# Layer 0's gate/up product in a hybrid streaming encoder step, rewritten as Strassen's seven block products

## The reference

```python
def swiglu(h, w_in, w_out):
    gu = h @ w_in
    return (jax.nn.silu(gu[..., :D_FF]) * gu[..., D_FF:]) @ w_out

hp = hp + rms_norm(swiglu(rms_norm(hp, g[2]), ffn_w_in[layer], ffn_w_out[layer]), g[3])
```

## Time and profile before

| | |
|---|---|
| median of 3 runs | 1019.76 us (1017.18 to 1019.86) |
| profiled execution, first to last instruction | 1018.8 us |
| TensorE busy | 1003.2 us, 98% |
| VectorE busy | 627.9 us, 62% |
| ScalarE busy | 518.8 us, 51% |
| DMA | 161.77 MB, 159 GB/s over the span |
| mean granted TensorE clock | 0.997 of full |

### The profile page before, as it was taken

How to read it: one execution, slowest core, us unless ns; L and a number is a source line. 1 busy time by engine, 2 the same in 40 slices (tenths; PEclk the granted TensorE clock), 3 DMA queues, 4 the chain that set the end, 5 groups by cost and what they waited for, 6 DMA issues and landing times.

```text
span 1018.8 us, 18393 instructions
## 1 busy us (share of the span) xinstructions
PE 1003.2 (98%) x7578; PEld 972.6 (95%) x7578; DVE 627.9 (62%) x918; ACT 518.8 (51%) x902; POOL 48.4 (5%) x55
## 2 busy tenths in 40 slices
PE   7999999999999999999999999999999999999997
PEld 6799899999999999999999999999999999999886
DVE  5396655878555555544579778798855555444553
ACT  5633665655444444444457655676544444444442
POOL 0081210000000000000000000001000000000000
PEclk9999999999999999999999999999999999999999
DMA  8322131666665555546655476556655555456653
GB/s 277 82 79 84 42 101 46 185 195 180 187 186 169 164 166 165 166 133 182 185 157 162 143 202 196 166 150 203 186 171 166 165 166 155 135 163 178 211 168 134
DMA packets 290516, 161.77 MB, mean 159 GB/s; under 512 B 14522, under 2 KB 281634, under 8 KB 290432
## 3 DMA queue, kind: packets, MB, share of 16 engines
q1 hardware_dynamic: 289968, 160.13, 53.9%
q0 software_dynamic: 224, 0.35, 0.1%
q10 hardware_dynamic: 240, 0.10, 0.0%
HBM read 157.98 MB, written 2.58 MB: 158 GB/s over the span
## 4 chain that ended last, share of the span: by engine, by line
PE 89%; DVE 6%; DMA 2%; ACT 2%; issue 1%; DVEq 0%; ACTq 0%
PE ps L564 29%; PE ps L566 28%; PE ps L565 28%; DVE wlo L1551 2%; DVE tmp L1827 1%; ACT whi L1089 1%; DMA raw<-in_ffn_w_out_dram 1%; DMA gain_rows<-in_norm_g_dram 1%; PE ps L815 1%; PE ps L759 1%; PE ps L650 1%; DMA raw<-in_ffn_w_in_dram 0%; DVE tmp L1813 0%; DMA raw<-in_c_w_dram 0%; DVE h L1817 0%
## 5 line engine op out<-in xcount | busy, mean ns | idle before, releaser
L1551 DVE TENSOR_TENSOR wlo<-raw,whi 128x1024 fp32r<-128x1024 f32 (+2 forms) x322 | 366.4, 1140 | 261.5 <-ACT whi L1089 261.2
L564 PE MATMUL ps<-xhi,whi 128*128 128x256 f32 (+1 forms) x1600 | 466.6, 292 | 1.4 <-DVE xlo L1836 0.9
L566 PE MATMUL ps<-xhi,wlo 128*128 128x256 f32 (+1 forms) x1600 | 460.8, 288 | 0.0
L565 PE MATMUL ps<-xlo,whi 128*128 128x256 f32 (+1 forms) x1600 | 459.8, 287 | 0.0
L1089 ACT ACTIVATE whi<-raw 128x1024 fp32r<-128x1024 f32 (+2 forms) x322 | 313.9, 977 | 224.6 <-PE ps L566 190.9
L564 PEld LDWEIGHTS ps<-xhi,whi 128*128 128x128 f32 x1600 | 300.9, 188 | 3.9 <-issue 2.1
L565 PEld LDWEIGHTS ps<-xlo,whi 128*128 128x128 f32 x1600 | 301.1, 188 | 0.0
L566 PEld LDWEIGHTS ps<-xhi,wlo 128*128 128x128 f32 x1600 | 300.9, 188 | 0.0
L564 PE MATMUL ps<-mhi_b,whi 128*128 128x288 f32 x352 | 105.5, 300 | 0.0
L566 PE MATMUL ps<-mhi_b,wlo 128*128 128x288 f32 x352 | 105.0, 298 | 0.0
L565 PE MATMUL ps<-mlo_b,whi 128*128 128x288 f32 x352 | 103.5, 294 | 0.0
(11 more groups left out here) (234 smaller groups left out, 1029.0 us busy)
## 6 DMA issues: line engine op xcount, KB each, us to landing
raw<-in_ffn_w_in_dram SPq DMA_DIRECT2D x176, 512.0 KB, 3.8
raw<-in_ffn_w_out_dram SPq DMA_DIRECT2D x48, 384.0 KB, 3.4
raw<-in_ffn_w_out_dram SPq DMA_DIRECT2D x48, 320.0 KB, 3.1
raw<-in_ffn_w_out_dram SPq DMA_DIRECT2D x22, 512.0 KB, 4.4
raw<-in_ab_w_in_dram SPq DMA_DIRECT2D x10, 512.0 KB, 5.4
raw<-in_ab_w_out_dram SPq DMA_DIRECT2D x10, 256.0 KB, 2.8
raw<-in_ab_w_out_dram SPq DMA_DIRECT2D x20, 128.0 KB, 3.2
x_tok<-in_x_prompt_dram SPq DMA_DIRECT2D x4, 512.0 KB, 7.4
```

Of the source, the lines that this page charges most:

```text
L564: pe.matmul(out, wh, xh, start=first, stop=False)
L565: pe.matmul(out, wh, xl, start=False, stop=False)
L566: return pe.matmul(out, wl, xh, start=False, stop=last)
L1551: dve.tensor_tensor(wlo[:, s, 0:n], raw[:, m % NRAW, 0:n], whi[:, s, 0:n].bitcast(F32), ALU.subtract)\
```

## The change

Layer 0's gate/up product no longer runs as two halves of the frames with all weights each. Frames (halves 0 and 1), model width (blocks k 0 to 3 and 4 to 7) and columns (gate and up of the same f) make it a 2 x 2 by 2 x 2 block product, done with seven block products of half the depth and half the frames:

- First pass, `fast_first`: unit p(f), the gate weights of f on half 0, in two halves of the depth. The first half's sum is copied to p1 (it is needed again), then the second half completes the gate of half 0. Meanwhile `combinations` builds the sums of x: S1, S2, S3, S4.
- Rest, `fast_rest`: for each f gate and up are loaded once more as a pair. VectorE makes four differences of their halves in t_sum (`first_terms`, `second_term`, `last_term`), split as units ta and tb; the second half of up is unit tc, split straight from `raw`. TensorE does five terms of 12 matmuls: S2 and S1 (ta), S3 (tb), S4 (tc of f - 1, `p3`), and the lower half of x (tb). ScalarE seeds PSUM with p1 (`seed`) and copies the running sum out twice (`keep_sum`); VectorE adds (`up_b`, `first_up`) and multiplies (`other_mult`, `first_mult`).
- `raw` has four slots, all four used by pairs and three by others; each pair takes two, so a pair lies in slots 2 and 3 and the next in 0 and 1.
- For b = 0 the gated values of f below 13 are split in the loop (`inner_high`, `inner_low`); the other nine blocks and all of b = 1 are split in ffn_out(0, 0) (`splits`).
- Small loads share semaphores: the gains wait for two loads, others for six and three. The stage table of (0, 1) is drawn together.

```diff
@@ constants and the table @@
-    (0, 1): {"sum": 1, "spread": 3, "scale": (3, 5, 7, 9), "fold": 11, "pre": 13, "again": 15, "x": (15, 17, 19, 21)},
+    (0, 1): {"sum": 0, "spread": 2, "scale": (2, 3, 4, 5), "fold": 6, "pre": 7, "again": 9, "x": (9, 10, 11, 12),
+             "s1": (11, 13), "s2": (14, 15, 16, 17), "s34": (17, 18)},
-NRAW, NSPLIT = 3, 4
+NRAW, NSPLIT = 4, 4
+FAST = (0,)
+EARLY = 13
@@ the order of the units @@
+        if layer in FAST:
+            seq += [("p", layer, f) for f in range(FC)]
+            for f in range(FC):
+                seq += [("ta", layer, f)] + [("tc", layer, f - 1)] * (f > 0) + [("tb", layer, f)]
+            seq.append(("tc", layer, FC - 1))
+LATE = [(f, min(f + 2, FC)) for f in range(EARLY, FC, 2)]
+PAIRS = [(f, f + 2) for f in range(0, FC, 2)]
+SPLIT_SLOTS = (0, 0, 0, 1, 1, *range(4, 26, 2))
@@ slots of raw @@
+        paired = load[0] in ("gate", "up")
+        if paired != (before in ("gate", "up")):
+            n = 2
+        slots.append(n)
+        holders.append(held[n])
+        held[n] = r
+        n = (n + 1) % (NRAW if paired else NRAW - 1)
...
-            def raw_free(m):
-                if m >= NRAW:
-                    sp.wait_ge(w_lo, m - NRAW + 1)
+            def raw_free(r):
+                if RAW_HOLDER[r] is None:
+                    if RAW_SLOT[r] == NRAW - 1:
+                        sp.wait_ge(w_used, U_OUT + len(OUT_DEPTHS))
+                    return
+                load = LOADS[RAW_HOLDER[r]]
+                if load[0] == "gate":
+                    sp.wait_ge(terms_done, terms(*load[1:]) + 3)
+                else:
+                    sp.wait_ge(w_lo, AT[("tc", *load[1:]) if load[0] == "up" else load] + 1)
@@ start @@
-            pe.wait_ge(gains_loaded, 16)
+            pe.wait_ge(gains_loaded, 32)
@@ TensorE, fast_first @@
+                for f, m in enumerate(P_PASS[layer]):
+                    pe.wait_ge(w_lo, m + 1)
...
+                    if f == 0:
+                        pe.wait_ge(x_lo_done[0], 8 * layer + 1)
+                        half_product(f, range(KC // 4), True, False)
+                        pe.wait_ge(x_lo_done[0], 8 * layer + 2)
+                        half_product(f, range(KC // 4, KC // 2), False, True).then_inc(p1_done, 1)
+                    else:
+                        half_product(f, range(KC // 2), True, True).then_inc(p1_done, 1)
+                        second(f - 1)
+                    run(f)
+                second(FC - 1)
@@ TensorE, fast_rest @@
+                def p3(f):
+                    m = AT["tc", layer, f]
+                    pe.wait_ge(w_lo, m + 1)
+                    pe.wait_ge(up_b_done, n0 + f + 1)
...
+                    term(m, 0, 2 + f % 2, *s4, CUT, False).then_inc(w_used, 1)
+                for f in range(FC):
+                    i = n0 + f
+                    ma, mb = AT["ta", layer, f], AT["tb", layer, f]
+                    pe.wait_ge(w_lo, ma + 1)
+                    pe.wait_ge(p1_seeded, i + 1)
...
+                    term(ma, HALF, f % 2, *s2, n, False).then_inc(sum_done, 1)
+                    if f >= 2:
+                        pe.wait_ge(up_a_done, i - 1)
...
+                    term(ma, 0, 2 + f % 2, *s1, n, True).then_inc(w_used, 1)
+                    pe.wait_ge(w_lo, mb + 1)
+                    pe.wait_ge(sum_kept, 2 * i + 1)
...
+                    term(mb, 0, f % 2, *s3, n, False).then_inc(sum_done, 1)
+                    if f:
+                        p3(f - 1)
+                    pe.wait_ge(sum_kept, 2 * i + 2)
+                    term(mb, HALF, f % 2, *a22, n, False).then_inc(w_used, 1)
+                p3(FC - 1)
@@ ScalarE, fast_rest @@
+                for f in range(FC):
+                    if f:
+                        gate_other(f - 1)
+                    else:
+                        s_high(layer, 3)
+                    if f < FC - 1:
+                        seed(layer, f + 1)
+                    inner_high(f - 2)
+                    keep_sum(f, 0)
+                    if f < FC - 1:
+                        hi_part(AT["ta", layer, f + 1])
+                    keep_sum(f, 1)
+                    hi_part(AT["tc", layer, f])
+                    if f < FC - 1:
+                        hi_part(AT["tb", layer, f + 1])
@@ VectorE @@
+            def first_terms(layer, f):
+                i = terms(layer, f)
+                g, u = LOAD_AT["gate", layer, f], LOAD_AT["up", layer, f]
+                dve.wait_ge(w_loaded[RAW_SLOT[g]], loaded(g))
+                dve.wait_ge(w_loaded[RAW_SLOT[u]], loaded(u))
...
+                dve.tensor_tensor(t[:, 0], pair_w[:, 1], pair_w[:, :, 0], ALU.subtract).then_inc(terms_done, 1)
...
+                for f in range(FC):
+                    lo_part(AT["tb", layer, f])
+                    if f:
+                        other_mult(f - 1)
+                    else:
+                        s_low(layer, 3)
+                    if f < FC - 1:
+                        first_terms(layer, f + 1)
+                    inner_low(f - 2)
+                    if f < FC - 1:
+                        second_term(layer, f + 1)
+                        lo_part(AT["ta", layer, f + 1])
+                        last_term(layer, f + 1)
+                    dve.wait_ge(sum_kept, 2 * (n0 + f) + 2)
+                    dve.tensor_tensor(up_b(f), e3(f), flat(2 + f % 2, 0, TOK - CUT), ALU.add).then_inc(up_b_done, 1)
+                    if f:
+                        first_up(f - 1)
+                    lo_part(AT["tc", layer, f])
+                    if f:
+                        first_mult(f - 1)
```

More of the change, by code:

```diff
@@ L117, in unit_sequence @@
     for layer in range(2):
-        for b in range(2):
+        if layer in FAST:
[3 more added lines that the diff above has]
+            seq.append(("tc", layer, FC - 1))
+        for b in range(2 if layer not in FAST else 0):
             for u in range(2 * FC):
@@ L147, in inner, with split_count @@
     return (2 * layer + b) * FC + f
+LATE = [(f, min(f + 2, FC)) for f in range(EARLY, FC, 2)]
+PAIRS = [(f, f + 2) for f in range(0, FC, 2)]
+SPLIT_SLOTS = (0, 0, 0, 1, 1, *range(4, 26, 2))
+def split_count(layer, b, f):
+    before = sum(SPLITS if n in FAST else 2 * FC for n in range(layer))
+    if layer not in FAST:
+        return before + b * FC + f + 1
+    if b:
+        return before + EARLY + len(LATE) + f // 2 + 1
+    return before + (f + 1 if f < EARLY else EARLY + (f - EARLY) // 2 + 1)
+SPLITS = EARLY + len(LATE) + len(PAIRS)
 def z_count(s, d):
@@ L177, in unit_columns, with load_sequence, load_of, raw_slots @@
     return UNIT
+def load_sequence():
+    seq = []
+    for unit in UNITS:
+        if unit[0] == "ta":
+            seq += [("gate", *unit[1:]), ("up", *unit[1:])]
+        elif unit[0] not in ("tb", "tc"):
+            seq.append(unit)
+    return seq
+LOADS = load_sequence()
+LOAD_AT = {load: r for r, load in enumerate(LOADS)}
+def load_of(m):
+    unit = UNITS[m]
+    return LOAD_AT[("up", *unit[1:]) if unit[0] == "tc" else unit]
+def raw_slots():
+    slots, holders, held = [], [], [None] * NRAW
+    n = 0
+    for r, load in enumerate(LOADS):
+        before = LOADS[r - 1][0] if r else load[0]
+        paired = load[0] in ("gate", "up")
[5 more added lines that the diff above has]
+        n = (n + 1) % (NRAW if paired else NRAW - 1)
+    return slots, holders
+RAW_SLOT, RAW_HOLDER = raw_slots()
+def terms(layer, f):
+    return 3 * (FAST.index(layer) * FC + f)
 def out_order(e):
     return [step for step, (_, b) in enumerate(OUT_STEPS) if b in (None, OUT_STEPS[e][1])].index(e)
[L185 to L194 removed]
+def load_dmas(r):
+    if U_IN + 6 <= r < U_IN + 10:
+        return 2
+    return 3 if LOADS[r][0] == "out" else 1
+def loaded(r):
+    return 16 * sum(load_dmas(j) for j in range(r + 1) if RAW_SLOT[j] == RAW_SLOT[r])
 def stepper(chain):
@@ L1508, in last_half, with splits @@
+            def splits(layer):
+                for step, slot in enumerate(SPLIT_SLOTS):
+                    yield slot
+                    split_high(layer, step)
             def last_half():
@@ new lines, in fast_first @@
+            def fast_first(layer, run):
+                for f, m in enumerate(P_PASS[layer]):
+                    run(f)
+                    if 0 < f < FC - 3:
+                        lo_part(m + 3)
+                    elif f == FC - 3:
+                        run(LAST)
+                        first_terms(layer, 0)
+                        second_term(layer, 0)
+                        lo_part(AT["ta", layer, 0])
+                    elif f == FC - 2:
+                        last_term(layer, 0)
@@ L2035, in pooling, with splits @@
+            def splits(layer):
+                for step, slot in enumerate(SPLIT_SLOTS):
+                    yield slot
+                    split_low(layer, step)
             def pooling(b):
```

527 lines of the change are left out of this document (424 added, 103 removed).

## The result

The changed kernel takes 1066.41 us (median of 4 runs, 1065.26 to 1068.35), the kernel before 1019.81 beside it (1017.18 to 1020.15): a ratio of 1.0471, 95% interval 1.0452 to 1.0491. The forecast was 1046, range 1032 to 1062. The sign came as forecast, and so did the closed loop behind it. The size did not: +46.6 us where +26 stood, and outside the range, most of it through a part that was costed at nothing.

What follows compares the result with a forecast made beforehand. TensorE, busy 98%, was taken as the bound. First pass to 253.8, then 12.25, 192.1, 13.8 and 5.0 give 477.0 against 451.6; with the front +26.0, span 1044.8, plus 1.0 for the median: 1046 us, range 1032 to 1062.

Steps and rivals of the forecast that it cites:

- the closed loop: In the rest, up's slot release, its next load and VectorE's chain from first_terms repeat every 10.18 us; 19 periods take 192.1.
- landing term: In the loop, the 512 KB load of up takes 3.70 us from issue to landing, once each period.
- rival 2: Up's load shares DMA engines with the load right behind: landing 4.8 us gives 1068 us, 4.2 gives 1056; chance 0.11.
- I cost this at nothing: In the first pass, VectorE's splits and 22 us of norm and combination work fit 29 us of room, adding nothing.
- The stop at 185: In the first pass, TensorE stands about 4 us ahead of sum_squares, until about 188.9.
- TensorE's stops of each turn: In the rest, TensorE idles about 2.3 us a period ahead of the last term, ended by ScalarE's copy.
- the turn from the end of the first pass to F2: From the first pass's end to the start of first_terms(2), including a load's landing: 12.25 us.
- the stop for the late splits: At the start of ffn_out, TensorE waits 3.3 us for late splits of gated values, plus 1.7 for the clock.
- F21 to the second product: From the start of first_terms(21) to the end of p3(21): 13.8 us.
- The front: At the kernel's start, gains_loaded also waits for scale_rows, delaying the transposition: 0.6 us taken, bounds 0 and 3.0.
- rival 1: The load is covered and VectorE paces the rest at 8.18 and 7.95 us: 154 for 19 periods, 1005 us; chance 0.08.
- Rival 4: The 2.3 us stops of each period keep TensorE's clock down: period 15.7 us, 1151 us in all; chance 0.04.

Runs made afterwards that it cites:

- Experiment 3: Changed kernel with VectorE making tc's low part, which frees up's slot, ahead of the two additions: 1052.45 us, ratio 1.0340 to the kernel before.
- experiment 4: Changed kernel with a buffer and load of its own for tc, so up's slot is free after second_term: 1014.83 us, ratio 0.9965 to the kernel before.
- (1): Changed kernel with the next gate load held back until first_terms has used up's load, so that load travels alone: 1064.1 us, ratio 1.0446.
- (2): Changed kernel with the next gate load held back and up read from gate's columns of the matrix: 1063.7 us, ratio 1.0453.
- 6: Changed kernel with weight slots dealt out from the second one on and the norm's second spread on TensorE one step earlier: 1058.99 us, ratio 1.0399.
- 5: Changed kernel with the four weight slots dealt out from the second one on, so gate(0)'s slot comes free one unit earlier: 1061.0 us, ratio 1.0424.
- the first version of experiment 10: Changed kernel with tc's own load, slots dealt from the second, VectorE's small steps behind second_term and ScalarE's table load behind late splits: 1004.15 us, ratio 0.9860.

## Why the prediction went wrong in size

**The loop held, its landing term was too short.** "Its period is 6.42 + 0.03 + 3.70 + 0.03": the 6.42 is 6.40, the 3.70 is 4.0 to 4.3. That is +9.0 us over 19 periods. By itself this would have stayed inside the range. Experiment 3 shows the one-for-one price and 4 shows that the loop is the cause of the loss: with it opened the kernel is faster than before. Of the 9.0, 3.2 come from the gate load right behind (1), at most 1.7 from where the columns lie (2), and 4.1 stay, most of them because a lone load took 3.8 to 4.0 and not 3.7. The prediction had this as rival 2, with 1056 at a landing of 4.2, and it took 3.7 because a load of 256 KB had kept its 2.8. That row was no evidence for a closed loop with 512 KB. x_tok's 4.2 with others 0.45 us behind the earlier trace rows was nearer in size and was set aside; but rival 2's mechanism, the load behind, makes only about 0.2 of the excess, so its 1056 for 4.2 would have been right partly by luck. The Trainium skill's "DMA: Bandwidth & Descriptors", section "Queues, rings and completion order", has each engine take one ring's descriptors in order. Read as in the prediction, that gives the first load no delay; the trace differs by 0.2 us and mostly agrees, since the load behind is the one that pays (5.3 to 5.6).

**The first pass: "I cost this at nothing" was the failed step**, +12.4 to +12.8 us, and the larger. The argument was one of sums: VectorE has 29 us of room for 22 us of work. It left out that this work comes behind waits. Without this term's miss the span would have come out near 1054, inside the range. Three ends were missed: the wait for the row factors with two splits queued behind it (6 has 2.5 us, at the edge of its interval), the first pair's load that sits behind the last splits of the pass and holds ScalarE's queue by way of second_term(0) (5 has 4.8, some 1.5 of which may be the clock), and the low clock behind each stop (0.83 in two windows, 3.0 us; one stop had been charged, not three; the cost differs from execution to execution). The stated price if the cover failed, "up to 1 us each, 2 or 3 times", was far too low, and it was not carried into the range. 5 us or more of this term are read from the windows alone; no run took them away one by one.

**What was right.** The stop at 185 (3.63, forecast to 188.9); TensorE's stops of each turn ahead of the last term (40.5 us over the stage, about 1.9 a turn where 2.3 was forecast); the turn from the end of the first pass to F2 (12.6, forecast 12.25); VectorE's second wait of 1.12 ahead of lo_part; the stop for the late splits, 2.83 against 3.3, with the clock at 0.83 behind it. F21 to the second product was 2.0 longer, 1.2 of it the clock (0.83, TensorE busy 7.22 in 480 to 490). The front cost 0.16 us, not 0.6: the first transposition moved from 6.78 to 6.94. The load that is covered, rival 1, was priced at 154 us for the 19 periods, and experiment 4 measured 153.8. Rival 4 (a clock that stays low) did not come: 0.95 in 284 to 464, and the period was bound elsewhere.

## What to carry to other kernels

When a change makes one buffer serve two users, draw the loop from "slot freed" through the load to the next use, and add it up. If it is longer than the engine's own turn, the landing is on the path, every tenth counts once a turn, and freeing the slot earlier is worth more than making anything faster; a copy of a quarter more bytes bought 5% here. Room in the sum of an engine's work is no cover: look for each wait in its queue, and ask what stands behind it that another engine wants. And where the path holds a landing, a kernel in which the loads are covered need not show its price (3.7 there; here 4.0 alone and 4.1 to 4.2 with a load behind), so let the range carry more than that row.

## What the runs showed of the hardware

- Two loads of 512 KB in one queue, 0.4 us apart: in 300 to 430 us the first lands in 4.0 to 4.3 us, the second in 5.3 to 5.6. Apart by 5 us they land in 3.9 to 4.2 and 3.7 to 4.1. The first is slowed a little by the one behind, about 0.2 us, the second by about 1.6.
- Where the load is covered, a landing of 4.9 us (median in 300 to 414, experiment 4) holds nothing up: the period is 8.1 us, with a quarter more bytes read for each f than in the kernel after. In 284 to 404 us the first version of experiment 10 moved 172 GB/s, the kernel before 171.
- How much low clock follows a stop of TensorE differs between executions of the same work. Behind the stop of 3.63 to 3.65 us near 188 the window 190 to 200 was at 0.71 to 0.89 in ten profiles. Behind the 1.76 us near 220 the window 220 to 230 was at 1.00 in eight profiles and at 0.83 to 0.85 in three. Behind the 4.60 to 5.20 us near 260 the window 260 to 270 was at 0.77 to 0.83 in all six. In the loop of the kernel after, stops of 2.45 to 2.64 us (303.64, 314.14, 324.83) stood in windows of 10 us at 1.00, and stops of 2.57 and 2.58 (356.79, 335.47) in windows at 0.87 and 0.85; the mean of 284 to 464 was 0.95. What tells them apart stays open.
